# Mixture-of-experts passes of a two-layer encoder: two fixed experts loaded first, a new pass order, and a last pass split around the reload of the outputs

## What is computed

```python
for l in range(DEPTH):                       # DEPTH = 2
    mod = (cond @ w_ada[l] + b_ada[l])[:, None, :]
    sh1, sc1, g1, sh2, sc2, g2 = jnp.split(mod, N_MOD, axis=-1)
    h = rms_norm(x, norm1[l]) * (1.0 + sc1) + sh1
    x = x + g1 * hybrid_mixer(h, ...)
    h = rms_norm(x, norm2[l]) * (1.0 + sc2) + sh2
    x = x + g2 * grouped_moe(h, w_router, router_bias, w1[l], w3[l], w2[l])
return rms_norm(x, norm_f)
```

## Time and profile before

| | us |
|---|---|
| median of the runs | 1576.4 (1575.21 to 1576.48) |
| profiled execution, its own time | 1578.35 |
| its span | 1576.5 |
| PE busy | 1476.3, 94% of the span |
| VectorE busy | 575.3, 36% |
| ScalarE busy | 427.8, 27% |
| mean granted TensorE clock | 0.972 of full |

### The profile page before, as it was taken

The page is one execution under the profiler, slowest core; times in us unless marked ns, Lnnn a source line. Parts: engine busy times, 40 slices in busy tenths (PEclk is TensorE's granted clock), DMA queues, the critical chain, the costliest instruction groups (busy, mean ns, idle before and its releaser), DMA issues.

```text
span 1576.5 us, 19611 instructions
## 1 busy us (share of the span) xinstructions
PE 1476.3 (94%) x7572; PEld 801.5 (51%) x7573; DVE 575.3 (36%) x1343; ACT 427.8 (27%) x980; POOL 86.9 (6%) x96
## 2 busy tenths in 40 slices
PE   5998999999999699999989899999999949999996
PEld 1664555677754333444346555666776423334442
DVE  0056554575643401111154464463333250111115
ACT  2326564300012112111141565551000121111111
POOL 0000002000000001000000000020000000111000
PEclk8999999999999699999999999999999969999998
DMA  9625163225260799999962432501304239999994
GB/s 361 231 82 201 43 228 120 81 66 148 67 253 27 298 418 422 420 422 423 381 238 107 140 132 89 179 1 41 106 1 165 83 139 419 420 419 423 421 409 174
DMA packets 94872, 346.83 MB, mean 220 GB/s; under 512 B 13722, under 2 KB 37882, under 8 KB 80376
## 3 DMA queue, kind: packets, MB, share of 16 engines
q1 hardware_dynamic: 69152, 305.68, 49.5%
q0 software_dynamic: 8976, 31.46, 5.4%
q10 hardware_dynamic: 16648, 8.40, 1.8%
HBM read 331.55 MB, written 21.00 MB: 224 GB/s over the span
## 4 chain that ended last, share of the span: by engine, by line
PE 87%; DMA 5%; DVE 4%; ACT 2%; issue 1%; DVEq 1%; SPq 0%; POOLq 0%; ACTq 0%
PE bank L2035 18%; PE bank L1773 12%; PE bank L1723 10%; PE bank L2046 9%; PE bank L1941 7%; PE bank L1815 7%; PE bank L1830 5%; PE bank L1840 4%; PE bank L1850 4%; DMA ring<-in_w 2%; PE bank L1756 2%; PE bank L1654 2%; PE bank L1687 2%; PE bank L2001 1%; DMA ring<-in_w_ada 1%
## 5 line engine op out<-in xcount | busy, mean ns | idle before, releaser
L2035 PE MATMUL bank<-ring,reg_b 128*32 128x512 f32 (+2 forms) x1376 | 284.3, 609 | 3.0 <-ACT reg_b L1082 3.0
L2035 PEld LDWEIGHTS bank<-ring,reg_b 128*32 128x32 f32 (+2 forms) x1376 | 94.2, 129 | 141.5 <-issue 137.2
L1723 PE MATMUL bank<-ring,hT 128*128 128x512 f32 (+3 forms) x512 | 159.2, 472 | 2.4 <-ACT hT L915 2.4
L1723 PEld LDWEIGHTS bank<-ring,hT 128*128 128x128 f32 x512 | 97.8, 192 | 59.3 <-issue 32.5
L2046 PE MATMUL bank<-ring,reg_b 128*32 128x512 f32 (+2 forms) x576 | 127.3, 594 | 0.0
L1815 PE MATMUL bank<-reg_a,ring 128*128 128x512 f32 x256 | 112.6, 593 | 0.9 <-issue 0.9
L1941 PE MATMUL bank<-ring,reg_b 128*128 128x512 f32 x256 | 113.0, 596 | 0.0
L1082 ACT ACTIVATE reg_b<-bank,cur 128x128 f32<-128x128 f32 x176 | 64.0, 469 | 177.6 <-PE bank L2001 177.6
L994 ACT ACTIVATE reg_f<-bank,nmax 128x512 f32<-128x512 f32 x128 | 87.2, 685 | 61.4 <-DVE nmax L1292 60.3
L1292 DVE TENSOR_REDUCE nmax<-bank 128x1 f32<-128x512 f32 x128 | 83.7, 685 | 51.2 <-PE bank L1830 51.2
L1773 PE MATMUL bank<-hT,ring 128*128 128x256 f32 x384 | 88.1, 379 | 0.0
(11 more groups left out here) (292 smaller groups left out, 1812.1 us busy)
## 6 DMA issues: line engine op xcount, KB each, us to landing
ring<-in_w SPq DMA_DIRECT2D x76, 2048.0 KB, 23.3
ring<-in_w_ada SPq DMA_DIRECT2D x19, 2048.0 KB, 7.4
ring<-in_w_in SPq DMA_DIRECT2D x10, 2048.0 KB, 19.1
hT<-in_w SPq DMA_DIRECT2D x10, 2048.0 KB, 27.9
reg_a<-in_w SPq DMA_DIRECT2D x10, 2048.0 KB, 21.6
vb<-in_w_ada ACTq DMA_DIRECT2D x16, 512.0 KB, 4.0
ring<-in_w_o SPq DMA_DIRECT2D x4, 2048.0 KB, 8.6
ring<-in_w_proj_a SPq DMA_DIRECT2D x8, 512.0 KB, 10.7
```

Of the source, the lines that this page charges most:

```text
L1723: ins = pe.matmul(bank[z_bank(k)][:, 0:n], hT[:, c, t * P:(t + 1) * P], w[:, c, :], start=c == 0, stop=c == NC - 1)
L2035: ins = pe.matmul(bank[bk][at:at + n, :], xsT[:, p % 2, c, at:at + n], slot(MOE_SLOT[j, m], NC, F)[:, c, :], start=c == 0, stop=c == NC - 1)
```

## The change

Five things change, all in or around the passes.

- Two fixed experts. Places 0 and 1 are now the experts 11 and 12, with 96 rows each. A constant added to their counts makes them rank 14 and 15 whatever the router gives (`C_KE`), so all 16 experts go through the ranking: its tiles grow from 15x15 to 16x16.
- Loads. Six loads come before the wait for `ord_s` instead of three: all weights of places 0 and 1. The others follow in a new order with new slots and new waits.
- Pass order. `TILES` and `EXPERT_RANK` are new. The last pass has one place (15) instead of two, pass 9 has three.
- The last pass on PE: up with w1, down product of pass 9, up with w3, own hidden transposes, own down product. On DVE `put_out(9)` moves between the two multiplications of the hidden rows.
- The reload of the outputs is issued before the count for extra blocks is read. `cy[0]` and `cy[1]` wait for the scatter and for the down product of pass 9, `cy[2]` and `cy[3]` for the last w3 product too. DVE adds them before it takes out the last pass. If extra blocks run, the outputs are loaded once more and the rows beyond the limit are added with weights of their own (`gw_over`). After layer 1, x goes into the PE accumulation for all four blocks of tokens (`fx_s`), ScalarE squares and DVE scales straight from the banks.

```diff
@@ 
 PASSES = 11
-EXPERT_RANK = (None, 13, 5, 6, 7, 8, 9, 10, 0, 1, 11, 12, 2, 3, 4, 14)
-TILES = (((0, 0, 32), (0, 32, 32), (0, 64, 32), (1, 96, 32)),
...
-         ((14, 0, 32), (14, 32, 32), (14, 64, 32), (15, 96, 32)))
+STATIC = (11, 12)
+EXPERT_RANK = (14, 15, 9, 0, 4, 5, 10, 1, 8, 13, 2, 6, 7, 11, 12, 3)
+TILES = (((0, 0, 32), (0, 32, 32), (0, 64, 32), (1, 96, 32)),
+         ((1, 0, 64), (2, 64, 64)),
+         ((3, 0, 128),),
+         ((4, 0, 32), (4, 32, 32), (4, 64, 32), (5, 96, 32)),
...
+         ((12, 0, 64), (13, 64, 32), (14, 96, 32)),
+         ((15, 0, 128),))
@@ constants
+    for k, e in enumerate(STATIC):
+        c[:, C_KE + e] = -4 * E * SEQ * (k + 1)
@@ SP, before the order of the experts is known
-                load_w1(0, 0)
-                load_w3(0, 0)
+                load_w2(0, STATIC[0])
+                load_w1(1, STATIC[1])
                 wait(sp, ya_r, l * 8 + 8)
-                load_w2(0, 0)
+                load_w2(1, STATIC[1])
+                wait(sp, yb_r, l * 8 + 8)
+                load_w1(0, STATIC[0])
+                wait(sp, wo_r, l * 8 + 8)
+                load_w3(0, STATIC[0])
+                wait(sp, lp4_r, l * NT + NT)
+                load_w3(1, STATIC[1])
 
                 wait(sp, ord_s, l + 1)
@@ SP, the end of a layer's passes
+                wait(sp, h1_r, l * PASSES + 10)
+                load_w1(15, rank[15])
+                wait(sp, h1_r, l * PASSES + 10)
                 load_w2(13, rank[13])
                 wait(sp, h1_r, l * PASSES + 10)
                 load_w2(14, rank[14])
+                wait(sp, h3_r, l * PASSES + 10)
+                load_w3(15, rank[15])
+                wait(sp, h3_r, l * PASSES + 10)
+                load_w2(15, rank[15])
                 if l < DEPTH - 1:
                     wait(sp, h3_r, l * PASSES + 10)
                     load_z(l + 1, 0)
-                wait(sp, h1_r, l * PASSES + 11)
-                load_w2(15, rank[15])
-                if l < DEPTH - 1:
+                    wait(sp, y_r, (l * PASSES + 9) * 2)
                     load_z(l + 1, 1)
-                    wait(sp, h3_r, l * PASSES + 11)
+                    wait(sp, h1_r, l * PASSES + 11)
                     load_z(l + 1, 2)
+
+                def load_outputs(t, done):
+                    sp.dma_start(cy[t].rearrange("p k n -> p (k n)"), ys_d.rearrange("(t p k) n -> t p (k n)", p=P, k=2)[t]).then_inc(done, 16)
+                for b in range(2):
+                    wait(sp, ys_st[b], (l + 1) * (16 * scatters(b)))
+                wait(sp, y_r, (l * PASSES + PASSES - 1) * 2)
+                for t in range(2):
+                    load_outputs(t, cg_s[t])
+                wait(sp, h3_r, l * PASSES + PASSES)
+                for t in range(2, NT):
+                    load_outputs(t, cg_s[t])
@@ DVE, passes
-                    if e < PASSES:
-                        hidden(l * PASSES + e)
-                    if e >= 1:
+
+                    def out_before():
                         if e >= 3:
                             v.wait_ge(ys_st[(e - 1) % 2], l * (16 * scatters((e - 1) % 2)) + 16 * ((e - 1) // 2))
                         put_out(e - 1, (e - 1) % 2)
+                    if e == PASSES - 1:
+                        hidden(l * PASSES + e, between=out_before)
+                    elif e < PASSES:
+                        hidden(l * PASSES + e)
+                        if e >= 1:
+                            out_before()
+                    else:
+                        add_outputs(l, 0)
+                        out_before()
+                        if l < DEPTH - 1:
+                            add_output(l, 1, 0)
@@ DVE, after the last layer
+            v.drain().then_inc(fx_s, 1)
             for t in range(NT + 1):
...
+                if t + 1 < NT:
+                    add_outputs(DEPTH - 1, t + 1).then_inc(fx_s, 1)
                 if t:
                     u = t - 1
-                    mean_square(2 * DEPTH, u)
+                    v.wait_ge(sqh_s, DEPTH + t)
+                    TS(lsum[:, u:u + 1], lsum[:, u:u + 1], 1.0 / D, EPS, ALU.mult, ALU.add)
+                    v.drain()
+                    v.wait_ge(sq_s, 2 * DEPTH * NT + t)
+                    TS(ssq[:, u:u + 1], ssq[:, u:u + 1], 1.0 / D, lsum[:, u:u + 1], ALU.mult, ALU.add).then_inc(ms_s, 1)
...
-                    STT(xn[:, u, :], x[:, u, :], rstd[:, u:u + 1], nf_row, ALU.mult, ALU.mult).then_inc(out_s, 1)
+                    for h in range(2):
+                        cols = slice(h * 512, (h + 1) * 512)
+                        ins = STT(xn[:, u, cols], bank[last_bank(DEPTH - 1, u) + h][:, :], rstd[:, u:u + 1], nf_row[:, cols], ALU.mult, ALU.mult)
+                    ins.then_inc(out_s, 1)
@@ PE, passes
                     for m, done in ((0, h1_r), (1, h3_r)):
+                        if p == PASSES - 1 and m == 1:
+                            pe.wait_ge(tr_e, g)
+                            pe.wait_ge(y_e, (l * PASSES + p - 1) * 2)
+                            down_tiles(p - 1)
                         for j in places(p):
                             loaded(j, m)
...
-                    if p >= 1:
+                    if 1 <= p < PASSES - 1:
```

More of the change, by code:

```diff
@@ L74, in rows_by_rank @@
             r = EXPERT_RANK[j]
-            if r is not None:
-                first[r] = p * P + at if first[r] is None else first[r]
-                rows[r] += n
+            first[r] = p * P + at if first[r] is None else first[r]
+            rows[r] += n
     return first, rows
-MOE_LOADS = ((0, 0, 0), (0, 1, 1), (0, 2, 2), (1, 0, 3), (1, 1, 4), (2, 0, 5), (3, 0, 6),
[6 rows of a table removed]
+MOE_LOADS = ((0, 2, 0), (1, 0, 1), (1, 2, 2), (0, 0, 3), (0, 1, 5), (1, 1, 6),
[7 rows of a table added]
 MOE_SLOT = {(j, m): s for j, m, s in MOE_LOADS}
@@ L169, in constants @@
     first, rows = rows_by_rank()
-    for p, tiles in enumerate(TILES):
-        for j, at, n in tiles:
-            if EXPERT_RANK[j] is None:
-                c[:, C_ST + STATIC + j] += n
-                c[:, C_ST + j] = P * p + min(a for i, a, _ in tiles if i == j)
-    c[:, C_BC:C_BC + RANKED] = first
-    c[:, C_BC + RANKED:C_BC + 2 * RANKED] = rows
+    c[:, C_BC:C_BC + E] = first
+    c[:, C_BC + E:C_BC + 2 * E] = rows
     return c
@@ L482, in trunk @@
         cg_s = [sem(f"token_outputs_loaded{t}") for t in range(NT)]
+        cx_s = [sem(f"token_outputs_with_extra_blocks_loaded{l}") for l in range(DEPTH)]
+        fx_s = sem("final_x_in_sbuf")
         ov_free = sem("extra_block_done")
@@ L510, in wait, with extra_blocks @@
             eng.sem_inc(ticks, 1)
-        def extra_blocks(eng, blocks, tables, body, new_table=None):
+        def extra_blocks(eng, blocks, tables, body, new_table=None, finish=None):
             most = eng.value_load(flag_i[0:1, 0:1], min_val=0, max_val=SEQ)
@@ L763, in body, with all_outputs @@
                     sp.dma_start(slot(5, 4, D), w2_v[l * E + e]).then_inc(ov_w, 16)
+                def all_outputs():
+                    wait(sp, ov_all, l + 1)
+                    for t in range(NT):
+                        load_outputs(t, cx_s[l])
                 wait(sp, fl_s, l + 1)
-                extra_blocks(sp, n_ov, n_tab, body)
-                for b in range(2):
-                    wait(sp, ys_st[b], (l + 1) * (16 * scatters(b)))
-                wait(sp, ov_all, l + 1)
-                wait(sp, h3_r, l * PASSES + PASSES)
-                for t in range(NT):
-                    sp.dma_start(cy[t].rearrange("p k n -> p (k n)"), ys_d.rearrange("(t p k) n -> t p (k n)", p=P, k=2)[t]).then_inc(cg_s[t], 16)
+                extra_blocks(sp, n_ov, n_tab, body, finish=all_outputs)
                 wait(sp, y_r, (l * PASSES + PASSES) * 2)
@@ L867, in body @@
                     wait(pool, ov_free, n + 1)
+                    for t in range(2, NT):
+                        wait(pool, cg_s[t], l * 16 + 16)
                     pool.tensor_copy(idx[:, 0:1], table[:, bass.ds(e, 1)]).then_inc(ov_i, 1)
@@ L1116, in _ @@
             for t in range(NT):
-                act.wait_ge(x2, DEPTH * NT + t + 1)
-                square(2 * DEPTH, t)
+                for h, (total, done) in enumerate(((lsum, sqh_s), (ssq, sq_s))):
+                    act.wait_ge(lp_r, ((DEPTH - 1) * NT + t) * 2 + h + 1)
+                    A(sq_j[:, h * 512:(h + 1) * 512], bank[last_bank(DEPTH - 1, t) + h][:, :], ACT.Square,
+                      accum_out=total[:, t:t + 1]).then_inc(done, 1)
                 root(2 * DEPTH, t)
@@ L1553, in _, with hidden @@
                 v.tensor_copy(flag_i[:, :], r_s[0:1, 160:161]).then_inc(fl_s, 1)
-                def hidden(at):
+                def hidden(at, between=None):
                     v.wait_ge(sge_s, at + 1)
                     TT(u_s, bank[4][:, :], sg_e, ALU.mult)
+                    if between is not None:
+                        between()
                     v.drain()
@@ L1660, in last_pass @@
                     pe.wait_ge(wt_s, layer + 1)
```

(6 more changed lines are left out.)

204 lines of the change are left out of this document (95 added, 109 removed), and 13 rows, old and new, of the table MOE_LOADS.

## The result

| | before | after |
|---|---|---|
| median of the runs | 1576.4 | 1626.3 (1623.59 to 1626.6) |
| profiled execution | 1578.35 | 1626.06 |
| its span | 1576.5 | 1624.2 |
| mean granted TensorE clock | 0.972 | 0.976 |

A forecast was written before the change was run, and what follows sets the result against it. In layer 0's passes PE's work and the weight transfers were taken to have the same length. +1.0 us at layer 0's end and -2.7 at layer 1's gave -1.7 on 1576.4: 1574.7 us, "the same", range 1569.5 to 1580.

The forecast's parts named there:

- Part 3: New pass order: PE's work unchanged, a stall of 0.5 us in each layer at w2 of place 14 (0 to 3).
- Rival C: More tokens than rows, so extra blocks run in the layer: near 50 us more, 1626; chance 0.02.
- Rival A: Transfers 1.5% slower: reload late at layer 0's end, costing 4.2 us, layer 1 +0.3; 1580.9; chance 0.14.
- Part 1: Routing: DVE tiles grow from 225 to 256 elements, costing +0.3 us in each layer.
- Part 2: Six early loads: pass 1's waits go, gaining 0.7 us in layer 0, 0.3 in layer 1, net of part 1.
- Part 4: End of layer 0: block 0 lands at 787.5, then 10.9 us to the transposes at 798.4, +1.0 us.
- Part 5: End of layer 1: pass 10 loses 1.1 us, DVE's list ends at 1570.7; 1573.8 against 1576.5, -2.7 us.

The follow-up runs named there:

- best of both: Kernel before with the new end of the layer, projection loads 1 and 2 behind the reload: 1575.59 us, ratio 0.9977; measured again 1573.75 us, 0.9971.
- two sizes in the kernel before: Kernel before with place 2 in pass 1 cut as tiles of 64 and 32 rows instead of three of 32: 1625.16 us, ratio 1.0294.
- sizes one after the other: Changed kernel, each product running all chunks of the 32-column tiles first, then those of the 64-column tile: 1611.01 us, ratio 1.0205 to the kernel before.
- one tile size: Changed kernel with the 64-row tile of place 12 in pass 9 written as two of 32: 1581.59 us, ratio 1.0026 to the kernel before.
- one size, projection loads behind: Changed kernel with pass 9 in tiles of 32, projection loads 1 and 2 behind the reload: 1576.59 us, ratio 0.9991 to the kernel before.
- one size, copies first: Changed kernel with pass 9 in tiles of 32, layer 0's `put_out(10)` ahead of block 0's additions: 1579.68 us, ratio 1.0005 to the kernel before.
- end of the layer alone: Kernel before with only the split last pass, early reload and layer 1's sums on PE; own experts, passes and loads: 1581.46 us, ratio 1.0025.
- loads and passes alone: Kernel before with new fixed experts, passes (pass 9 in tiles of 32) and load order; own last pass, reload and sums: 1591.91 us, ratio 1.0083.
- all three projection loads behind: Kernel before with the new end of the layer and all three projection loads behind the reload: 1572.76 us, ratio 0.9969.

## Why the prediction was wrong

The layer in two pieces shows it best. For layer 0, the time from the first of the routing's eight tile instructions to the first product of the next layer's projection (515.75 to 802.21 before); for layer 1, from the same instruction to the end of the span (1279.94 to 1576.5). Differences to before, each from one profiled execution. The same kernel can differ by 2 us and more between two of them ("best of both" stands here twice):

| kernel | layer 0 | layer 1 |
|---|---|---|
| before | 286.5 | 296.6 |
| forecast | +1.0 | -2.7 |
| changed | +23.2 | +24.0 |
| changed, less 26.8 for pass 9 | -3.6 | -2.8 |
| two sizes in the kernel before | +20.9 | +23.9 |
| sizes one after the other | +16.1 | +17.6 |
| one tile size | +4.4 | +0.4 |
| one size, projection loads behind | -1.7 | 0.0 |
| one size, copies first | +1.7 | -0.1 |
| end of the layer alone | +3.0 | -3.2 |
| loads and passes alone | +4.8 | +9.4 |
| best of both | -2.2 | -2.5 |
| best of both, second execution | -4.5 | -2.9 |
| all three projection loads behind | -4.5 | -3.0 |

**Part 3 failed**, in the sentence "The number of one-place passes stays four, so PE's work doesn't change". It counted places per pass and not the sizes of their tiles. The description of the kernel before, that a pass of four tiles takes about the time of a pass of one, was true for every pass that its trace showed, because 96 rows were always three tiles of 32. The new table has the first pass with two sizes, and nothing in the rows covered it: a case for a bound, not for zero. Serial groups would have given up to 14 us for the up products and 7 for the down product as the upper end, 42 us over both layers, and the term was carried as 0 without a range. The experiments with the size mix taken out, put in elsewhere and grouped settle this part.

**Rival C's number is a coincidence.** It gave 1626, for an extra block of experts. No instruction of such a block ran in either layer; the forecast's chance of 0.02 for that mechanism says nothing on the cause found.

**Rival A is close to what is left without the size mix.** It said 1580.9: layer 0 4.2 later, layer 1 +0.3. With one tile size the chip gave 1.0026, which is 1580.5 on 1576.4, with +4.4 and +0.4 in the trace. That the 4.4 meets the 4.2 is partly luck. Forecast and rival count to the transposes, and there the kernel with one size is 6.3 later (801.60 - 513.62 against 797.43 - 515.75). The piece from there to the product took 4.78 us before, at a granted clock of 0.59 (797 to 802.5), and 2.88 now, at 1.00, which gives 1.9 back. Its mechanism, the slower transfers, is there. The stretch in which its transfers are saturated, first in the kernel with one size, then in the kernel before (columns as in the earlier trace rows):

```profile
567.40:763.40 196.00, 193.68 (x1162) 75.28 (x1160) 24.80 (x36) 36.64 (x90) 16.17 (x16) 1.00 1.01 414
```
```profile
561.70:763.20 201.50, 201.35 (x1028) 80.62 (x1032) 25.39 (x37) 36.32 (x89) 16.18 (x16) 1.00 1.01 421
```

414 against 421 GB/s, 1.7% less; the rival had 1.5%. The kernel with the new end alone, on the same chip as the one with one size but with the old order, has 421 too (561.70 to 763.20). From the landing of w2 of place 2 to that of the last w2 there are 37 loads in 206.0 us, 5.57 each; with loads and passes alone it is 206.5; before, 40 loads took 217.7, 5.44 each. So it comes with the new order of loads and passes. PE then waits at four places for w2, where one wait of 0.5 in each layer was forecast: 0.66 and 1.84 us in layer 0, 0.96 and 1.63 in layer 1. The last of each layer:

```profile
1532.05 0.62 PE L2083 MATMUL bank<-ring,reg_b 128*32 128x512 f32 x2 [1.63 <-DMA hT<-in_w]
```

The loss lies in the first part of the stretch. Of the kernel with one size (columns as above):

```profile
620.00:640.00 20.00, 20.00 (x121) 7.05 (x124) 2.42 (x4) 4.10 (x10) 2.03 (x2) 1.00 0.99 378
640.00:760.00 120.00, 119.34 (x737) 47.00 (x730) 14.53 (x21) 21.10 (x51) 10.07 (x10) 1.00 1.01 421
```

From 640 on it moves 421 GB/s, as before (420); from 570 to 620 it is 412 against 421, and from 620 to 640 it is 378 against 424. Between 617.8 and 627.2 only one or two weight loads are on their way at a time; before, three or four are. A scatter and a gather run beside them in both, from 621 and from 624 on. Over 570 to 760 a load into `ring` took 15.7 us from issue to landing (median) where before it took 25.0. So the missing bytes fall where few loads stand in the queue. No run changes that number alone, so the cause is not shown. The changed kernel itself hides all of this behind the 26.8 us.

**Part 1** held: from the first tile instruction to the slot table's product, 7.28 us in place of 6.98. The forecast was +0.3.

**Part 2** held in its main point. The early loads don't shorten the saturated stretch: w2 of place 2 landed at 568.2 in the changed kernel, where 569.3 was forecast and everything ahead of the experts ran 1.5 earlier, so 0.4 off. The wait for weights at pass 1 is gone. What was missed is that the gather of the first tokens now runs beside more of the expert loads. In layer 0 it took 5.92 to 6.70 us in the six executions with the early loads and 5.34 to 5.91 in the six without them; in the changed kernel:

```profile
524.13 6.70 DMA reg_b<-xn_d,table
```

From the routing to the end of pass 1's products the changed kernel gained 0.0 in layer 0 (53.13 against 53.17) and 0.6 in layer 1, where 0.7 and 0.3 were forecast.

**Part 4** had the right chain and a wrong landing. In the changed kernel the reload came early and the end of layer 0 was bound by PE:

```profile
804.86 7.13 PE L2083 MATMUL bank<-ring,reg_b 128*128 128x512 f32 x16 [0.69 <-ACT reg_b L1106]
...
805.66 2.65 DVE L1165 SCALAR_TENSOR_TENSOR x<-reg_a,gw,x 128x1024 f32<-128x1024 f32 x2 [2.20 <-DMA reg_a<-ys_d]
...
812.03 0.69 DVE L1586 TENSOR_TENSOR reg_d<-bank,reg_c 128x512 f32<-128x512 f32 x1 [2.67 <-PE bank L2083]
...
814.26 5.29 PE L1706 MATMUL bank<-reg_d 128*128 128x512 f32 x8 [2.27 <-issue]
```

That is the -3.6 of the table, with the 1.9 us of the clock behind the transposes in it; at the transposes it is -1.7. With one size the case of the forecast is real: block 0 lands 275.4 after the first routing row (789.06 - 513.62), where 271.8 was forecast, 3.7 late by the slower transfers. From there to the transposes it took 12.6 us, not 10.9. The 1.7 is TensorE's clock, 0.50 of full from 790 to 798: the first four matmuls of L1706 took 3.80 us where 1.85 was taken, and all eight, 3.70 in the earlier trace rows, took 5.29 to 6.51 in six of the traces (below). The exposed piece ahead of the last down product was forecast at 2.3 and is 804.86 - 802.75 = 2.1.

**Part 5** had the right number on another chain. In the changed kernel the last down product ends at 1600.57, which is 296.9 - 26.8 = 270.1 after the routing row; forecast 270.6. From there to the end 23.6 us, forecast 23.3, and before it was 27.1. But the forecast has VectorE's list as what bounds this end, 18.6 us after the count, with PE's groups beside it. The chain goes through PE:

```profile
1602.56 1.58 PE bank L1705 x2
...
1617.37 0.87 PE bank L1706 x2
...
1618.26 0.70 ACT reg_f L1131 x2
```

PE adds up the four blocks without a gap from 1602.56 to 1618.24, 15.7 us where 14.8 was taken, and the last block's squares and norm follow. Its first three pieces took 4.5 us instead of 2.6, at a granted clock of 0.72 (1602 to 1608). VectorE is busy for 14.9 of the 19.1 us from 1602.04 to the end of its last scaling, so its list was taken too long, and PE's work, which was taken to be hidden, ends last. That both sums lie so close is luck. With one size the sums are the same (23.7), and the waits for w2 take 2.6 us of the gain in place of 0.5.

So parts 1 and 2 held in the main, part 5 met its number on another chain, part 4 was off by 3 to 5 us through the transfers' rate and TensorE's clock, and a term that was not costed, in part 3, decided the result.

## What to carry to other kernels

Before tiles of TensorE are cut anew, list for each pass which column sizes run in it. One size per pass costs what one full pass costs; two sizes cost two passes and the changes between them. Merging three tiles of 32 columns into 64 + 32 saves instructions and here more than doubled the time of the pass (31.83 + 15.88 us against 13.87 + 7.0). And a term that the trace of before can't show, because no pass of that kind exists there, gets its upper end from the nearest serial case, not zero.

For a tail of this kind: what is needed first goes first on the queue. Here a reload queued behind 2.5 MiB of projection weights took 5 us longer; with the weights behind the reload, PE did not wait for either.

## What was not expected of the hardware

Tiles with 32 columns run side by side with each other (four in 0.87 us per chunk), and tiles with 64 with each other (pass 1 of the changed kernel, 13.95 us), but not with the other size: 1.99 us per chunk, of which 0.27 is for the two changes.

TensorE's granted clock fell to half (0.50, which is 1.2 instead of 2.4 GHz) after gaps at the end of layer 0 in eight of the twelve traces, and not at the same place. With one tile size, the stretch from 790 to 798, the last part of 7.4 us of idling and the groups behind it, shows 0.50. In the best version it is 1.00 there, and the fall lies in the last down product instead. Even this does not hold for the kernel as such: a second execution of the same kernel shows no fall from 770 to 830. Here is the stretch with the last down product, first in the first execution, then in the second (columns as in the earlier trace rows):

```profile
780.00:790.00 10.00, 8.94 (x66) 2.85 (x64) 3.20 (x4) 2.08 (x3) 0.00 (x0) 0.83 0.82 324
```
```profile
780.00:790.00 10.00, 7.62 (x66) 2.67 (x66) 5.12 (x7) 1.04 (x2) 0.00 (x0) 1.00 0.98 393
```

The clock was 0.83 and 1.00 of full in them, and the last down product took 8.8 and 7.1 us. PE had been busy for 2.3 of the 4 us ahead of it in the first and for 1.8 in the second, so the one with less idling is the one that shows the fall. Likewise the same eight matmuls of the sums took 5.40 us at a clock of 0.72 (projection loads behind the reload, 790 to 796) and 3.70 at 1.00. A duration near such a gap is good to 1.7 us only, between kernels and between two executions of one, and an effect of that size is read from the medians of several runs, not from one trace.
